# Spread of the row factors in two passes, with the rounded diagonal from ScalarE and its rest from VectorE

## The chip, the cores and the metric

The kernel runs on one core of one Trainium2 chip. The metric is the device time of one execution in microseconds (us). Three runs of the kernel before took 1000.03, 1002.32 and 1002.96 us; their median, 1002.32 us, is its time.

## The reference, cut to what matters

One layer of an encoder: 512 rows of width 1024, all in float32.

```python
def _rms(x, g):
    y = x * lax.rsqrt(jnp.mean(x * x, axis=-1, keepdims=True) + EPS)
    return y * g

x = x + 0.5 * _swiglu(_rms(x, g_ffn1), w_up1, w_down1)      # macaron half-step
h = _rms(x, g_mix)
z = h @ w_in                                                # q, k, v, f, gates
x = x + (gate_a * y_a + gate_b * y_b) @ w_out               # attention and Fourier branches
x = x + 0.5 * _swiglu(_rms(x, g_ffn2), w_up2, w_down2)      # macaron half-step
out = _rms(x, g_final)
```

What matters here is the factor of `_rms`: each of the 512 rows has one number, 1/sqrt(mean of its squares + EPS). The change concerns how that number reaches all 128 partitions.

## The kernel before, in words

**Layout.** `xT` holds x transposed: the model dimension lies on the partitions, the 512 rows along the free dimension. A product therefore has the rows of x as its 512 columns, and the factor of a row has to be known on every partition. The kernel multiplies the raw, gained x (`h_hi`, `h_lo`) by the weights first and applies the factor to the result, in `gate(r, d)` (L1072) and `up(r, d)` (L1078), from the tile `rstd` (128x512, every partition the same).

**Split products.** Operands are split in two: ScalarE rounds (`w_hi`, type float32r, L616), VectorE subtracts (`w_lo`, L1010). TensorE makes three passes for each 128x128 tile: hi by hi (L1556), hi by lo (L1557), and then, once `w_lo` is there, lo by hi (L1568). A granule is 8 such tiles, that is 24 passes of 512 columns. Four slots hold four granules; SP loads granule g when VectorE has split granule g - 4.

**Factors.** There are four norms: `NORM_FFN1` before the first half-step, `NORM_MIX` before the mixer, `NORM_FFN2` before the second half-step, `NORM_FINAL` at the end (it does not use the step changed here). For the first three:

- `sum_squares(n)` on TensorE sums the squares over the partitions into one bank, a row of x on each partition;
- `mean(n)` on VectorE (L1047) makes `var`, GpSimd (L1506) raises it to the power -1/2 and has `rinv`, 128x4: one column for each block of 128 rows;
- `diagonal(n)` on VectorE (L1035) writes `ident * rinv[:, t]` into the four 128-column blocks of `gb_t`;
- `spread_factors(n)` on TensorE (L1599) multiplies a 128x128 tile of ones by it, in plain float32, so that every partition of the bank holds all 512 factors;
- `factors(n)` on VectorE (L1041) copies the bank to `rstd`.

**Where they stand.** The order on each engine is written out by hand. In the half-steps (r = 0 for the first, r = 1 for the second) TensorE runs granules 0 to 3, the `sum_squares` after granule 2 and the `spread_factors` inside granule 3, between its hi passes and its lo passes. Then comes granule 4, which waits until `gate(r, 0)` has read its bank (`out_read`). VectorE's order in `direct_pairs(r)` is

```python
direct_lo(r, 4); mean(nrm); direct_lo(r, 5); diagonal(nrm)
direct_lo(r, 6); factors(nrm); gate(r, 0); up(r, 0); gate(r, 1); up(r, 1); swish(r, 0)
```

ScalarE's order there is `direct_hi` 4, 5 and 6, then `silu(r, 0)` and `silu(r, 1)` (L687), then `direct_hi` 7. In the mixer the granules of f are `f_rows(0)` to `f_rows(3)` (L1772, L1773, L1777); `sum_squares` follows `f_rows(0)`, `spread_factors` follows `f_rows(1)`. There ScalarE splits granule `G_F + 4` after the first and has nothing to do until the second is done.

`gate_t` is the pair `ga_t`, `gb_t`; both are free while the factors are made.

Of the kernel before, what the change touches and what calls it, by code (L numbers as in the profile page):

```python
# [19 lines left out]
F32 = mybir.dt.float32  # L20
F32R = mybir.dt.float32r
ACT = mybir.ActivationFunctionType
ALU = mybir.AluOpType

P = 128
SEQ, D_MODEL, D_FF = 512, 1024, 2816
# [10 lines left out]
TB = SEQ // P  # L37
# [217 lines left out]
def build(nc, io):  # L255
# [9 lines left out]
    with ExitStack() as ctx:  # L265
# [39 lines left out]
        p1_t, _, p1_size = place("p1_t", [P, 2, HALF], F32, ssum_at)  # L305
        u2_t, _, u2_size = place("u2_t", [P, 2, HALF], F32, ssum_at + p1_size)
        u3_t, _, _ = place("u3_t", [P, HALF], F32, ssum_at + p1_size + u2_size)
        ga_t, _, _ = place("ga_t", [P, SEQ], F32)
        gb_t, _, _ = place("gb_t", [P, SEQ], F32)
        ua_t, ua_at, _ = place("ua_t", [P, SEQ], F32)  # L310
        ub_t, _, _ = place("ub_t", [P, SEQ], F32)

# [8 lines left out]
        y_t, _, _ = place("y_t", [P, SEQ], F32)  # L321
        rows = y_t
        ident, _, _ = place("ident", [P, P], F32)
        ones, _, _ = place("ones", [P, P], F32)
        assert at[0] % (TILE_AT // 2) == 0

        a_hi, act_at, a_size = place("a_hi", [P, FK * SEQ], F32R)
# [54 lines left out]
        def sem(name):  # L382
            return ctx.enter_context(nc.semaphore(name))
# [24 lines left out]
        w_lo_ready, h_lo_ready, x_ready = sem("w_lo_ready"), sem("h_lo_ready"), sem("x_ready")  # L408
        out_read, product_ready, a_lo_ready = sem("out_read"), sem("product_ready"), sem("a_lo_ready")
        gain_ready, consts_ready, row_ready = sem("gain_ready"), sem("consts_ready"), sem("row_ready")  # L410
        var_ready, diag_ready, rstd_ready = sem("var_ready"), sem("diag_ready"), sem("rstd_ready")
        proj_lo_ready, v_lo_ready, tab_lo_ready = sem("proj_lo_ready"), sem("v_lo_ready"), sem("tab_lo_ready")
        v_hi_ready = sem("v_hi_ready")
        s_read, max_ready, den_ready, probs_ready = sem("s_read"), sem("max_ready"), sem("den_ready"), sem("probs_ready")
# [199 lines left out]
        def _(act):  # L614
# [3 lines left out]
            def split_hi(g, it=0, n=0):  # L618
# [16 lines left out]
                    act.wait_ge(w_used, g - SLOTS + 1 + n * it)  # L635
                copy(w_hi[:, s, 0:nk, :], raw[:, s, 0:nk, :]).then_inc(w_hi_ready, 1)

            def square_free(n, m):

                if not isinstance(m, int) or m >= 3:  # L640
                    act.wait_ge(sum_added, m + ((DK - 1) * n - 2))
# [14 lines left out]
            act.dma_start(gain_rows[:, :], io["g_ffn1"][0].rearrange("(r p) -> r p", p=P)).then_inc(gain_landed, 16)  # L656
            act.wait_ge(fills_ready, 1)

            nc.scalar.activation(warm[:, :], ones[:, 0:2], ACT.Silu)

            act.wait_ge(gain_ready, 1)

# [17 lines left out]
            def direct_hi(r, j):  # L680

                split_hi(G_UP[r] + j)
# [5 lines left out]

            def direct_pairs(r):

                for j in (4, 5, 6):
                    direct_hi(r, j)
                silu(r, 0)
                silu(r, 1)
                direct_hi(r, 7)
                if r == 0:
                    act.wait_ge(row_ready, 1)
                    act.dma_start(bias_rows, bias_row[:, :]).then_inc(bias_stored, 16)
                t_rounded(r, T_B11)
                direct_hi(r, 8)  # L700
                t_rounded(r, T_1)
                t_rounded(r, T_B21)
                direct_hi(r, 9)
                t_rounded(r, T_2)
                silu(r, 2)
                t_rounded(r, T_4)
                direct_hi(r, 10)
                t_rounded(r, T_3)
                t_rounded(r, T_B22)
                silu(r, 3)  # L710
                direct_hi(r, 11)
                group_hi(r, 0, G0)
                silu(r, 4)
                group_hi(r, 0, G1)
                group_hi(r, 0, G2)
                silu(r, 5)
# [122 lines left out]
            for r in range(2):  # L839
# [19 lines left out]
                for step in mixer_schedule(MIXER_SCALAR):  # L859
                    kind = step[0]  # L860
                    if kind == "f":
                        grp = step[1]
                        if grp == N_FGROUPS - 1:
# [4 lines left out]
                            for nth, i in enumerate((0, 2, 1, 3)):  # L868
                                act.wait_ge(uv_formed, nth + 1)
                                copy(uv_hi[:, i, :], uv_of(i)).then_inc(uv_hi_ready, 1)  # L870
                        split_hi(G_F + grp + SLOTS)
                        if grp == 1:
                            act.wait_ge(tables_landed, 16)
                            copy(tab_hi[:, :], tab_raw[:, :]).then_inc(tab_hi_ready, 1)
# [127 lines left out]
        def _(dve):  # L1002
# [28 lines left out]
            def diagonal(n):  # L1031

                dve.wait_ge(rinv_ready, n + 1)
                for t in range(TB):
                    last = vec.tensor_scalar(gb_t[:, t * P:(t + 1) * P], ident[:, :], rinv[:, t:t + 1], None, ALU.mult)  # L1035
                last.then_inc(diag_ready, 1)

            def factors(n):

# [428 lines left out]
            for h in range(2):  # L1468
# [11 lines left out]
                t = 2 * h  # L1480
# [5 lines left out]
        @block.gpsimd  # L1486
        def _(pool):
            nc.gpsimd.memset(ident[:, :], 0.0).then_inc(ident_ready, 1)
            pool.wait_ge(ident_ready, 1)
            nc.gpsimd.affine_select(out=ident[:, :], in_=ident[:, :], compare_op=ALU.not_equal, fill=1.0, base=0,  # L1490
                                    pattern=[[-1, P]], channel_multiplier=1).then_inc(ident_ready, 1)
            nc.gpsimd.memset(ones[:, :], 1.0).then_inc(fills_ready, 1)
            nc.gpsimd.memset(half[:, :], -0.5).then_inc(fills_ready, 1)
            nc.gpsimd.memset(bias_row[:, :], NEG).then_inc(fills_ready, 1)
            pool.wait_ge(fills_ready, 3)
            for n in range(4):

                for m in range(1, DK - 1 if n == NORM_FINAL else DK):
                    pool.wait_ge(sq_ready, DK * n + m + 1)
                    if m > 1:  # L1500
                        pool.wait_ge(sum_added, (DK - 1) * n + m - 1)
                    nc.gpsimd.tensor_tensor(ssum[:, :], ssum[:, :], sq[:, m % 2, :], ALU.add).then_inc(sum_added, 1)  # L1502
                for i in range(2 if n == NORM_FINAL else 1):
                    blocks = slice(2 * i, 2 * i + 2) if n == NORM_FINAL else slice(0, TB)
                    pool.wait_ge(var_ready, n + 1 + i)
                    nc.gpsimd.tensor_tensor(rinv[:, blocks], var[:, blocks], half[:, blocks],  # L1506
                                            ALU.pow).then_inc(rinv_ready, 1)
                if n in (NORM_FFN1, NORM_FFN2):
                    r = 0 if n == NORM_FFN1 else 1
                    for i, (to, one, two) in enumerate(((T_1, T_B12, T_B11), (T_2, T_B22, T_1), (T_4, T_B21, T_2),  # L1510
                                                        (T_3, T_B22, T_B12))):
                        pool.wait_ge(normed, 2 * HK * r + (HK if to == T_1 else 2 * HK))
                        if i in (1, 2):
                            pool.wait_ge(t_formed, 4 * r + i)
                        nc.gpsimd.tensor_tensor(t_sum[:, to, :, :], t_sum[:, one, :, :], t_sum[:, two, :, :],
                                                ALU.subtract).then_inc(t_formed, 1)
                    for q in range(PAIRS):
                        blk = pair_raw[q % 2]
                        a12, a22 = blk[:, pair_slot(r, G1), 0:HK, :], blk[:, pair_slot(r, G1), HK:DK, :]
                        s2, s3 = blk[:, pair_slot(r, G0), HK:DK, :], blk[:, pair_slot(r, G2), HK:DK, :]  # L1520
                        pool.wait_ge(s13_ready, 2 * (PAIRS * r + q) + 1)
                        nc.gpsimd.tensor_tensor(s2, a22, s3, ALU.subtract).then_inc(s2_ready, 1)  # L1522
                        pool.wait_ge(s2_ready, PAIRS * r + q + 1)
                        nc.gpsimd.tensor_tensor(blk[:, pair_slot(r, G3), 0:HK, :], a12, s2,
                                                ALU.subtract).then_inc(s4_ready, 1)
# [3 lines left out]
        def _(pe):  # L1529
# [56 lines left out]
            def sum_squares(n):  # L1586

                pe.wait_ge(sum_added, (DK - 1) * (n + 1))
                if n == NORM_FFN1:
                    pe.wait_ge(x_ready, DK)  # L1590
                for t in range(TB):
                    mm = nc.tensor.matmul(banks[B_SUM[n]][:, 2 * t:2 * t + 2], ssum[:, t * P:(t + 1) * P], ones[:, 0:2],
                                          start=True, stop=True)
                mm.then_inc(sum_done, 1)

            def spread_factors(n):

                pe.wait_ge(diag_ready, n + 1)
                nc.tensor.matmul(banks[B_RSTD[n]][:, :], ones[:, :], gb_t[:, :], start=True, stop=True).then_inc(rstd_done, 1)  # L1599


            def x_tile(m):
# [9 lines left out]
            def warm_up(count):  # L1612

                for _ in range(count):
                    nc.tensor.matmul(banks[1][:, 0:P], ones[:, :], ones[:, :], start=True, stop=True)

            pe.wait_ge(fills_ready, 1)
            warm_up(6)
# [316 lines left out]
            def finish(h):  # L1935
# [4 lines left out]
                for last_one in (False, True):  # L1940
                    if last_one:
                        pe.wait_ge(last_squared, h + 1)
                    for t in (2 * h, 2 * h + 1):
                        squares = sq[:, 1, t * P:(t + 1) * P] if last_one else ssum[:, t * P:(t + 1) * P]
                        mm = nc.tensor.matmul(banks[B_SUM[NORM_FINAL]][:, 2 * t:2 * t + 2], squares, ones[:, 0:2],
                                              start=not last_one and t == 2 * h, stop=last_one and t == 2 * h + 1)
                mm.then_inc(sum_done, 1)
                pe.wait_ge(last_scaled, h + 1)
# [44 lines left out]
```

## Time and profile before

| | |
|---|---|
| median of three runs | 1002.32 us (1000.03 to 1002.96) |
| profiled execution, whole | 1004.33 us |
| its span, first to last instruction | 1002.5 us |
| mean granted TensorE clock | 0.992 of full speed |
| PE, VectorE, ScalarE, GpSimd busy | 98%, 68%, 44%, 20% of the span |

The profiled execution is one run of its own, so durations are read from it and compared with its own 1004.33 us; the 1.83 us beyond the span lie before the first and after the last instruction. PE is TensorE's matmul side, PEld its weight loads, DVE is VectorE, ACT is ScalarE, POOL is GpSimd, SP issues DMAs. A row of the timeline gives start, duration, engine, line, operation and tiles; "x4" are four instructions merged, with the time from the start of the first to the end of the last. A matmul's record is longer than its share of the array: passes start every 0.23 us while each is shown with 0.39 us. A plain float32 matmul shows as two records.

### The profile page before, as it was taken

The page shows a single profiled execution, that of the slowest core. Times are in us where ns is not written, and L with a number is a line of the kernel's source. Part 1 is how long each engine was busy: PE and PEld are TensorE (multiplying, and loading weights), DVE is VectorE, ACT ScalarE, POOL GpSimd, SP SyncE. Part 2 cuts the span into 40 slices and gives each one's busy share as a digit, 9 for nine tenths or more (in the row PEclk, how much of TensorE's full clock was granted, in tenths as well). Part 3 has the DMA queues.
Part 4 walks back from the last instruction along what each step waited for, and adds up shares of the span by engine and source line. Part 5 has one row for each costly group of instructions (what it writes and reads, how often), then busy time and mean ns, then how long its engine had stood idle before and what let it go on. Part 6 is the DMA issues. An engine that isn't in the chain of part 4 may idle for free.

```text
span 1002.5 us, 16130 instructions
## 1 busy us (share of the span) xinstructions
PE 986.5 (98%) x5780; PEld 876.0 (87%) x5780; DVE 681.4 (68%) x937; ACT 445.2 (44%) x667; POOL 197.8 (20%) x113
## 2 busy tenths in 40 slices
PE   8999999999999999899999999999999999999997
PEld 7789999999888888778888888888999999988887
DVE  6778898989544346568885555468899999953322
ACT  5344444446333234446775343334344444732322
POOL 2453343431011010000000002224233333001101
PEclk9999999999999999899999999999999999999999
DMA  6423333323432363112113343332243432342222
GB/s 212 121 70 105 102 108 99 110 84 90 116 100 89 112 168 117 54 44 83 52 54 108 102 126 104 94 103 58 85 121 90 116 93 84 89 130 87 89 68 84
DMA packets 188743, 98.26 MB, mean 98 GB/s; under 512 B 13384, under 2 KB 186520, under 8 KB 188704
## 3 DMA queue, kind: packets, MB, share of 16 engines
q1 hardware_dynamic: 186912, 94.45, 32.3%
q10 hardware_dynamic: 1792, 3.30, 0.9%
q8 instruction: 24, 0.39, 0.2%
q14 instruction: 15, 0.12, 0.0%
HBM read 95.61 MB, written 2.11 MB: 97 GB/s over the span
## 4 chain that ended last, share of the span: by engine, by line
PE 96%; POOL 1%; DMA 1%; issue 1%; DVE 1%; ACT 1%; SPq 0%; POOLq 0%; ACTq 0%
PE bank L1556 19%; PE bank L1557 19%; PE bank L1568 18%; PE bank L1671 11%; PE bank L1667 11%; PE bank L1665 11%; POOL ssum L1502 1%; PE bank L1871 1%; DMA x_rows<-in_x_dram 1%; PE bank L1772 1%; PE bank L1773 1%; PE bank L1777 1%; PE bank L1886 0%; PE bank L1858 0%; PE bank L1889 0%
## 5 line engine op out<-in xcount | busy, mean ns | idle before, releaser
L616 ACT ACTIVATE w_hi<-raw 128x1024 fp32r<-128x1024 f32 (+2 forms) x202 | 181.3, 901 | 236.9 <-PE bank L1568 148.0
L1010 DVE TENSOR_TENSOR w_lo<-raw,w_hi 128x1024 fp32r<-128x1024 f32 (+2 forms) x138 | 149.9, 1089 | 141.7 <-ACT w_hi L616 140.1
L1667 PE MATMUL bank<-t_lo,w_hi 128*128 128x256 f32 x896 | 224.7, 283 | 0.0
L1665 PE MATMUL bank<-t_hi,w_hi 128*128 128x256 f32 x896 | 224.6, 283 | 0.0
L1667 PEld LDWEIGHTS bank<-t_lo,w_hi 128*128 128x128 f32 x896 | 172.0, 192 | 0.2
L1665 PEld LDWEIGHTS bank<-t_hi,w_hi 128*128 128x128 f32 x896 | 172.0, 192 | 0.2
L1502 POOL TENSOR_TENSOR ssum<-ssum,sq 128x512 f32<-128x512 f32 x27 | 41.2, 1524 | 525.6 <-ACT sq L653 524.8
L1671 PE MATMUL bank<-t_hi,w_lo 128*128 128x256 f32 x896 | 144.0, 283 | 0.0
L1556 PE MATMUL bank<-a_hi,w_hi 128*128 128x512 f32 (+1 forms) x374 | 140.1, 379 | 0.0
L1557 PE MATMUL bank<-a_lo,w_hi 128*128 128x512 f32 (+1 forms) x374 | 139.4, 377 | 0.0
L1671 PEld LDWEIGHTS bank<-t_hi,w_lo 128*128 128x128 f32 x896 | 123.6, 192 | 0.0
L1178 DVE TENSOR_TENSOR w_lo<-raw,w_hi 128x1024 fp32r<-128x1024 f32 x64 | 90.9, 1420 | 9.3 <-ACT w_hi L616 9.3
L616 ACT ACTIVATE w_hi<-raw_b 128x1024 fp32r<-128x1024 f32 x64 | 60.8, 949 | 80.0 <-POOL raw_b L1522 40.3
L1178 DVE TENSOR_TENSOR w_lo<-raw_b,w_hi 128x1024 fp32r<-128x1024 f32 x64 | 92.8, 1450 | 3.8 <-ACT w_hi L616 3.7
L1568 PE MATMUL bank<-a_hi,w_lo 128*128 128x512 f32 (+1 forms) x374 | 91.1, 377 | 0.0
L1556 PEld LDWEIGHTS bank<-a_hi,w_hi 128*128 128x128 f32 x374 | 70.4, 188 | 12.9
L1557 PEld LDWEIGHTS bank<-a_lo,w_hi 128*128 128x128 f32 x374 | 70.4, 188 | 12.6
L1568 PEld LDWEIGHTS bank<-a_hi,w_lo 128*128 128x128 f32 x374 | 67.8, 188 | 12.9
L1556 PE MATMUL bank<-hf_hi,w_hi 128*128 128x512 f32 x192 | 76.5, 399 | 0.0
L1557 PE MATMUL bank<-hf_lo,w_hi 128*128 128x512 f32 x192 | 75.8, 395 | 0.0
L1556 PE MATMUL bank<-h_hi,w_hi 128*128 128x512 f32 x176 | 70.3, 399 | 0.4 <-issue 0.4
L1557 PE MATMUL bank<-h_lo,w_hi 128*128 128x512 f32 x176 | 69.9, 397 | 0.0
(238 smaller groups left out, 1488.1 us busy)
## 6 DMA issues: line engine op xcount, KB each, us to landing
raw<-in_w_down_dram SPq DMA_DIRECT2D x48, 384.0 KB, 3.0
raw_b<-in_w_up_dram SPq DMA_DIRECT2D x64, 256.0 KB, 3.7
raw<-in_w_up_dram SPq DMA_DIRECT2D x64, 256.0 KB, 3.6
raw<-in_w_up_dram SPq DMA_DIRECT2D x24, 512.0 KB, 3.8
raw<-in_w_in_dram SPq DMA_DIRECT2D x22, 512.0 KB, 3.7
raw<-in_w_down_dram SPq DMA_DIRECT2D x32, 128.0 KB, 2.2
raw<-in_w_out_dram SPq DMA_DIRECT2D x8, 512.0 KB, 3.4
x_rows<-in_x_dram SPq DMA_DIRECT2D x4, 512.0 KB, 7.9
```

What stands on the lines that cost most here:

```text
L616: return nc.scalar.activation(dst, src, ACT.Copy, scale=scale)
L1010: vec.tensor_tensor(w_lo[:, s, 0:nk, :], raw[:, s, 0:nk, :], w_hi[:, s, 0:nk, :].bitcast(F32), ALU.subtract).then_inc(w_lo_ready, 1)
L1178: vec.tensor_tensor(w_lo[:, slot, 0:nk, :], pair_raw[q % 2][:, slot, 0:nk, :], w_hi[:, slot, 0:nk, :].bitcast(F32), ALU.subtract).then_inc ...
L1502: nc.gpsimd.tensor_tensor(ssum[:, :], ssum[:, :], sq[:, m % 2, :], ALU.add).then_inc(sum_added, 1)
L1556: nc.tensor.matmul(out_ap, w_hi[:, s, k, :], xh, start=first and i == 0, stop=False)
L1557: mm = nc.tensor.matmul(out_ap, w_hi[:, s, k, :], xl, start=False, stop=False)
L1568: mm = nc.tensor.matmul(out_ap, w_lo[:, s, k, :], x_parts(k)[0], start=False, stop=last and i == len(tiles) - 1)
L1665: nc.tensor.matmul(out_ap, w_hi[:, slot, at_ + k, :], hi[:, k, :], start=first and k == 0, stop=False, skip_group_check=not first)
L1667: nc.tensor.matmul(out_ap, w_hi[:, slot, at_ + k, :], lo_[:, k, :], start=False, stop=False, skip_group_check=not first)
L1671: mm = nc.tensor.matmul(out_ap, w_lo[:, slot, at_ + k, :], hi[:, k, :], start=False, stop=k == HK - 1, skip_group_check=not first)
L1772: nc.tensor.matmul(o_ap, rows_of(h_hi, k, t), group_of_four(w_hi, slot, kk), start=k == 0, stop=False)
L1773: nc.tensor.matmul(o_ap, rows_of(h_lo, k, t), group_of_four(w_hi, slot, kk), start=False, stop=False)
```

## The change

The diagonal is made twice. ScalarE writes `ident * rinv` rounded to float32r into `diag_hi` (in the place of `ga_t`); VectorE writes the rest, `ident * rinv - diag_hi`, into `diag_lo` (in the place of `gb_t`). TensorE multiplies the ones, now of type float32r, by each, in one pass each that add up in the bank, in place of one float32 product. The second pass waits for the rest. In ScalarE's order the new step stands between `direct_hi` 5 and `direct_hi` 6 in both half-steps, and after the split of `G_F + 4` in the mixer. VectorE's step stays where it was and now waits for ScalarE's too. Other uses of the ones read them as float32, as before.

```diff
+        diag_hi, _, _ = place("diag_hi", [P, SEQ], F32R, ga_at)
+        diag_lo, _, _ = place("diag_lo", [P, SEQ], F32R, gb_at)
...
-        ones, _, _ = place("ones", [P, P], F32)
+        ones_r, _, _ = place("ones_r", [P, P], F32R)
...
+            def diagonal_hi(n):
+
+                act.wait_ge(rinv_ready, n + 1)
+                for t in range(TB):
+                    last = copy(diag_hi[:, t * P:(t + 1) * P], ident[:, :], scale=rinv[:, t:t + 1])
+                last.then_inc(diag_hi_ready, 1)
...
             def direct_pairs(r):
 
-                for j in (4, 5, 6):
-                    direct_hi(r, j)
+                direct_hi(r, 4)
+                direct_hi(r, 5)
+                diagonal_hi(NORM_FFN1 if r == 0 else NORM_FFN2)
+                direct_hi(r, 6)
                 silu(r, 0)
                 silu(r, 1)
                 direct_hi(r, 7)
...
                         split_hi(G_F + grp + SLOTS)
+                        if grp == 0:
+                            diagonal_hi(NORM_MIX)
...
             def diagonal(n):
 
                 dve.wait_ge(rinv_ready, n + 1)
+                dve.wait_ge(diag_hi_ready, n + 1)
                 for t in range(TB):
-                    last = vec.tensor_scalar(gb_t[:, t * P:(t + 1) * P], ident[:, :], rinv[:, t:t + 1], None, ALU.mult)
-                last.then_inc(diag_ready, 1)
+                    block = slice(t * P, (t + 1) * P)
+                    last = vec.scalar_tensor_tensor(out=diag_lo[:, block], in0=ident[:, :], scalar=rinv[:, t:t + 1],
+                                                    in1=diag_hi[:, block].bitcast(F32), op0=ALU.mult, op1=ALU.subtract)
+                last.then_inc(diag_lo_ready, 1)
...
             def spread_factors(n):
 
-                pe.wait_ge(diag_ready, n + 1)
-                nc.tensor.matmul(banks[B_RSTD[n]][:, :], ones[:, :], gb_t[:, :], start=True, stop=True).then_inc(rstd_done, 1)
+                pe.wait_ge(diag_hi_ready, n + 1)
+                nc.tensor.matmul(banks[B_RSTD[n]][:, :], ones_r[:, :], diag_hi[:, :], start=True, stop=False)
+                pe.wait_ge(diag_lo_ready, n + 1)
+                nc.tensor.matmul(banks[B_RSTD[n]][:, :], ones_r[:, :], diag_lo[:, :], start=False, stop=True).then_inc(rstd_done, 1)
```

## Rows read from the trace of the kernel before

**Rows 1.** The page's first part: busy time, share and instructions of each engine

```profile
PE 986.5 (98%) x5780; PEld 876.0 (87%) x5780; DVE 681.4 (68%) x937; ACT 445.2 (44%) x667; POOL 197.8 (20%) x113
```

**Rows 2.** The page's fourth part: the chain that ended last, by engine

```profile
PE 96%; POOL 1%; DMA 1%; issue 1%; DVE 1%; ACT 1%; SPq 0%; POOLq 0%; ACTq 0%
```

**Rows 3.** Waits of PE over the whole span: total us, times, longest

```profile
PE bank L1533 <- DVE y_t L1362: 2.3, 1, 2.3
```

**Rows 4.** Timeline of all engines around the spread of the second half-step

```profile
655.89 1.98 PE L1568 MATMUL bank<-hf_hi,w_lo 128*128 128x512 f32 x8
...
657.96 1.06 ACT L616 ACTIVATE w_hi<-raw 128x1024 fp32r<-128x1024 f32 x1 [4.38 <-PE bank L1568]
...
658.93 1.93 POOL L1506 TENSOR_TENSOR rinv<-var,half 128x4 f32<-128x4 f32 x1 [12.54 <-DVE var L1047]
659.04 1.28 ACT L687 ACT_TABLE_LOAD   x1
...
660.89 0.87 DVE L1035 TENSOR_SCALAR gb_t<-ident,rinv 128x128 f32<-128x128 f32 x4 [0.91 <-POOL rinv L1506]
...
661.68 1.22 DVE L1010 TENSOR_TENSOR w_lo<-raw,w_hi 128x1024 fp32r<-128x1024 f32 x1
...
662.28 1.02 PE L1599 MATMUL bank<-gb_t,ones 128*128 128x512 f32 x2
...
662.74 2.43 PE L1568 MATMUL bank<-hf_hi,w_lo 128*128 128x512 f32 x8
...
663.34 0.69 DVE L1041 COPY rstd<-bank 128x512 f32<-128x512 f32 x1 [0.44 <-PE bank L1599]
664.06 0.69 DVE L1072 TENSOR_TENSOR ga_t<-bank,rstd 128x512 f32<-128x512 f32 x1
...
665.00 0.40 PE L1556 MATMUL bank<-hf_hi,w_hi 128*128 128x512 f32 x1
```

**Rows 5.** Timeline around the spread of the first half-step

```profile
28.15 3.88 ACT L616 ACTIVATE w_hi<-raw 128x1024 fp32r<-128x1024 f32 x4
...
32.77 1.94 POOL L1506 TENSOR_TENSOR rinv<-var,half 128x4 f32<-128x4 f32 x1 [2.37 <-DVE var L1047]
...
37.52 1.02 PE L1599 MATMUL bank<-gb_t,ones 128*128 128x512 f32 x2
...
37.98 2.40 PE L1568 MATMUL bank<-hf_hi,w_lo 128*128 128x512 f32 x8
...
40.21 0.42 PE L1556 MATMUL bank<-hf_hi,w_hi 128*128 128x512 f32 x1
```

**Rows 6.** Timeline around the spread of the mixer

```profile
372.97 1.02 POOL L1506 TENSOR_TENSOR rinv<-var,half 128x4 f32<-128x4 f32 x1 [4.43 <-DVE var L1047]
...
376.64 1.02 PE L1599 MATMUL bank<-gb_t,ones 128*128 128x512 f32 x2
...
377.74 0.40 PE L1773 MATMUL bank<-w_hi,h_lo 128*128 128x512 f32 x1
```

**Rows 7.** ScalarE's groups by form: busy us and mean ns, then idle before

```profile
L616 ACT ACTIVATE w_hi<-raw 128x1024 fp32r<-128x1024 f32 x106 | 111.7, 1056 | 132.1 <-PE bank L1568 49.0 <-PE bank L1671 43.4 <-POOL raw L1522 25.1
...
L616 ACT ACTIVATE w_hi<-raw 128x512 fp32r<-128x512 f32 x48 | 29.6, 618 | 7.0 <-PE bank L1568 6.9
...
L616 ACT ACTIVATE hf_hi<-xT,consts 128x512 fp32r<-128x512 f32 x8 | 5.8, 723 | 25.8 <-DVE xT L1262 25.8
```

**Rows 8.** VectorE's groups by form, with the same columns

```profile
L1020 DVE SCALAR_TENSOR_TENSOR hf_lo<-xT,consts,hf_hi 128x512 fp32r<-128x512 f32 x8 | 6.0, 751 | 7.0 <-ACT hf_hi L616 7.0
...
L1361 DVE TENSOR_TENSOR y_t<-cos_t,bank 128x128 f32<-128x128 f32 x8 | 2.3, 281 | 0.1
```

**Rows 9.** Windows: from:to, length, busy by engine, PEclk, DMA share, GB/s

```profile
33.00:38.00 5.00, 5.00 (x17) 3.76 (x15) 2.83 (x6) 0.00 (x0) 1.71 (x1) 0.66 0.97 287
412.00:420.00 8.00, 6.84 (x20) 5.49 (x21) 4.01 (x12) 2.88 (x7) 0.00 (x0) 0.57 0.18 54
...
424.00:427.00 3.00, 0.99 (x9) 0.79 (x7) 2.92 (x4) 1.98 (x5) 0.00 (x0) 1.00 0.17 47
```

More of the change, by code:

```diff
@@ L307, in build @@
         u3_t, _, _ = place("u3_t", [P, HALF], F32, ssum_at + p1_size + u2_size)
-        ga_t, _, _ = place("ga_t", [P, SEQ], F32)
-        gb_t, _, _ = place("gb_t", [P, SEQ], F32)
+        ga_t, ga_at, _ = place("ga_t", [P, SEQ], F32)
+        gb_t, gb_at, _ = place("gb_t", [P, SEQ], F32)
+        diag_hi, _, _ = place("diag_hi", [P, SEQ], F32R, ga_at)
+        diag_lo, _, _ = place("diag_lo", [P, SEQ], F32R, gb_at)
         ua_t, ua_at, _ = place("ua_t", [P, SEQ], F32)
@@ L410, in build @@
         gain_ready, consts_ready, row_ready = sem("gain_ready"), sem("consts_ready"), sem("row_ready")
-        var_ready, diag_ready, rstd_ready = sem("var_ready"), sem("diag_ready"), sem("rstd_ready")
+        var_ready, rstd_ready = sem("var_ready"), sem("rstd_ready")
+        diag_hi_ready, diag_lo_ready = sem("diag_hi_ready"), sem("diag_lo_ready")
         proj_lo_ready, v_lo_ready, tab_lo_ready = sem("proj_lo_ready"), sem("v_lo_ready"), sem("tab_lo_ready")
@@ L657, in _ @@
             act.wait_ge(fills_ready, 1)
-            nc.scalar.activation(warm[:, :], ones[:, 0:2], ACT.Silu)
+            nc.scalar.activation(warm[:, :], ones_r[:, 0:2].bitcast(F32), ACT.Silu)
             act.wait_ge(gain_ready, 1)
@@ L1491, in _ @@
                                     pattern=[[-1, P]], channel_multiplier=1).then_inc(ident_ready, 1)
-            nc.gpsimd.memset(ones[:, :], 1.0).then_inc(fills_ready, 1)
+            nc.gpsimd.memset(ones_r[:, :].bitcast(F32), 1.0).then_inc(fills_ready, 1)
             nc.gpsimd.memset(half[:, :], -0.5).then_inc(fills_ready, 1)
@@ L1591, in sum_squares @@
                 for t in range(TB):
-                    mm = nc.tensor.matmul(banks[B_SUM[n]][:, 2 * t:2 * t + 2], ssum[:, t * P:(t + 1) * P], ones[:, 0:2],
+                    mm = nc.tensor.matmul(banks[B_SUM[n]][:, 2 * t:2 * t + 2], ssum[:, t * P:(t + 1) * P], ones_r[:, 0:2].bitcast(F32),
                                           start=True, stop=True)
@@ L1614, in warm_up @@
                 for _ in range(count):
-                    nc.tensor.matmul(banks[1][:, 0:P], ones[:, :], ones[:, :], start=True, stop=True)
+                    nc.tensor.matmul(banks[1][:, 0:P], ones_r[:, :].bitcast(F32), ones_r[:, :].bitcast(F32), start=True, stop=True)
             pe.wait_ge(fills_ready, 1)
@@ L1944, in finish @@
                         squares = sq[:, 1, t * P:(t + 1) * P] if last_one else ssum[:, t * P:(t + 1) * P]
-                        mm = nc.tensor.matmul(banks[B_SUM[NORM_FINAL]][:, 2 * t:2 * t + 2], squares, ones[:, 0:2],
+                        mm = nc.tensor.matmul(banks[B_SUM[NORM_FINAL]][:, 2 * t:2 * t + 2], squares, ones_r[:, 0:2].bitcast(F32),
                                               start=not last_one and t == 2 * h, stop=last_one and t == 2 * h + 1)
```

## The prediction, made before the changed kernel was run

> **What bounds the kernel now.** I read the page's busy shares first: TensorE is busy 98% of the span, no other engine above 68% [rows 1]. The chain that ended last is TensorE for 96% [rows 2]. So what counts is TensorE's time, and what other engines do counts only where TensorE waits for it. The waits of PE come third: the dearest on another compute engine is one of 2.3 us in the mixer [rows 3], and none lies at the three places that the change touches. Then the timeline of those three places, since a wait that is not there now may be there afterwards; it shows how close the present order is. In the second half-step `gate` ends at 664.06 + 0.69 = 664.75 us and granule 4, which waits for it, starts at 665.00 [rows 4]: 0.25 us of room, no more. Last the windows, for the granted clock.
>
> **TensorE's saving.** Passes of 512 columns start every (1.98 - 0.39)/7 = 0.227 us at full clock (eight passes of L1568 in 1.98 us, the last one's record 0.39) [rows 4]. The float32 product in the second half-step starts at 662.28. Behind it stand eight passes and then granule 4's first at 665.00: 2.72 us, of which the eight passes are 1.82, so the product holds the array for 0.90 us. In the first half-step the same sum is 40.21 - 37.52 - 1.82 = 0.87 [rows 5], in the mixer 377.74 - 376.64 - 0.23 = 0.87 [rows 6]. Two float32r passes take 0.45. The saving is at most 0.42 us at each place, 1.3 us in all, if nothing is late.
>
> **The new instructions.** They are four ScalarE copies of 128 columns with a scale from a tile, and four scalar_tensor_tensor of 128 columns on VectorE in place of four tensor_scalar. The trace shows neither form.
> ScalarE: the copy with such a scale is 723 ns at 512 columns; a column costs (1056 - 618)/512 = 0.86 ns [rows 7]; for 128 columns that gives 0.723 - 384 x 0.00086 = 0.395 us. Instructions back to back overlap by (4 x 1.056 - 3.88)/3 = 0.115 [rows 5, 7]. Four take 4 x 0.395 - 3 x 0.115 = 1.24 us.
> VectorE: 0.751 at 512 columns; a column of a two-tensor operation costs (1.22 - 0.281)/896 = 1.05 ns (w_lo of 1024, y_t of 128) [rows 4, 8], which gives 0.348 for 128. The overlap is (4 x 0.281 - 0.87)/3 = 0.085, taking a tensor_scalar at y_t's 281 ns [rows 4, 8]. Four take 1.14 us.
> The bounds for each four are 0.87, which the present four take, and four 512-column instructions end to end, 2.9 and 3.0 us. I stay with 1.24 and 1.14, since the 128-column rows are the nearest.
> The Trainium skill ("VectorE: DVE Perf Modes", section "The DRAIN you can't avoid") says that the next VectorE instruction starts only when the pipe is empty, which speaks against cutting work in four. Here four of about 281 ns end after 0.87 us, so the trace shows some overlap [rows 4, 8]. Without any overlap the eight would take 2.97 us in place of 2.38, and the second half-step would lose 0.6 us more.
>
> The two fours lie one behind the other: `rinv`, then ScalarE 1.24, then VectorE 1.14; before, only 0.87 lay there. Behind the new ScalarE step stands `direct_hi` 6, which so far ran long before; behind VectorE's stand `direct_lo` 6, the copy to `rstd`, and `gate`.
>
> **First half-step.** `rinv` ends at 34.71 [rows 5]. Rounded diagonal 34.76 to 36.00, rest 36.03 to 37.17. TensorE wants them at 37.52 and 37.75: no stall, since it runs at a reduced clock just before (0.66 mean over 33 to 38 us) [rows 9]. `w_hi` 6 is ready at 36.95, `w_lo` 6 at 38.3, the copy starts at 38.2 (the second pass ends at 37.75 + 0.39), `gate` about 0.73 later (as 663.34 to 664.06) [rows 4] and ends at 39.64; with 0.2 for hand-over and restart of TensorE, granule 4 can start at 39.84. By TensorE's own work it would be 39.79. Before it was 40.21. Term: -0.37 us. If the diagonals are cheaper, -0.42; at the far end (VectorE 3.0) +2.
>
> **Mixer.** `rinv` ends at 373.99 [rows 6]; diagonals ready at 375.3 and 376.45, wanted at 376.64 and 376.87. Behind ScalarE's wait stands the split of the next granule, which waits for TensorE's end of `f_rows(1)` anyway. Term: -0.42 us; its cover is 0.4 us thick, and it turns to +1.3 at the far end.
>
> **Second half-step.** Here TensorE runs at full clock and the cover is gone. `rinv` ends at 660.86 [rows 4]. Rounded diagonal to 662.14, rest from 662.17 to 663.31. TensorE wants the rest at 662.28 + 0.23 = 662.51 and stalls until about 663.4: 0.9 us, half of it paid by the saving. But that is not what ends last. `w_hi` 6, which before ran at 657.96, now ends at 663.1. `w_lo` 6 starts behind the rest, 663.23, and ends at 664.45 (before 662.90); copy from 664.37; `gate` 665.09 to 665.77; granule 4 with the 0.2 at 665.97 in place of 665.00. Term: +0.97 us, nothing of the saving left. With 0.87 for each four it is +0.5; with no overlap +1.6; at the far end +3.3 with VectorE's 3.0. The table load of 1.28 us that followed `w_hi` 6 at 659.04 now runs from 663.1 to 664.4, still ahead of `gate`'s end: no cost [rows 4]. The SP load that waits for `w_lo` 6 comes 1.6 us later, for a granule four granules of 24 x 0.227 = 5.4 us away: no cost. No wait of PE follows in this half-step before its last rows, so nothing gives the time back: all engines there move with TensorE.
>
> **Sum.** -0.37 - 0.42 + 0.97 = +0.2 us. On the profiled execution's own time that is 1004.33 + 0.2 = 1004.5; on the median of the runs, which lies 2 us lower, 1002.5 us. The bounds of the costs alone give -0.3 (each four 0.87) to about +6.6 (the three far ends), and +1.2 when only the overlap is missing.
>
> **Rivals.**
> A. Nothing is late in the second half-step, since ScalarE starts its four earlier or does them much faster than its rows say: 1.3 us are saved, 1001.0 us. For it: TensorE is the bound. Against: even 0.87 for each four leaves the rest late, at 662.6, and `gate` behind it. 0.08.
> B. Slower: the stall of 0.9 us and the one at granule 4 behind it put TensorE at half clock, as it is in 412 to 420 us after the wait in the mixer. There the granted clock is 0.57 (a mean over the two levels, 2.4 and 1.2 GHz), and (1 - 0.57) x 8 = 3.4 us of full-speed work are lost [rows 3, 9]. It would give 1002.5 + 3.4 = 1005.9. Against: in 424 to 427 TensorE is busy for only 0.99 us of 3 and keeps its full clock [rows 9]. It decides from the point where a short stall is followed by a second one. 0.07. The Trainium skill ("TensorE: Matmul & The Clock Gate", section "HAM oscillation — how this bites in real kernels") has idle gaps bring the half clock back. The trace shows both outcomes.
> C. The other way round: a stretch at half clock falls away because work has shifted by half a microsecond. The stretch around 33 to 38 us costs (1 - 0.66) x 5 = 1.7 us, the one in the mixer 3.4 [rows 9]: 999 to 1001 us. The three runs of the kernel before lie 2.9 us apart, so something of this size comes and goes by itself. 0.05.
> D. The float32r passes of the spread cost as much as the float32 product. Then the savings are gone, 0.8 us more: 1003.3. Against: all other float32r passes of that size start every 0.227 us. 0.02.
> The forecast's own case has the remaining 0.78.
>
> **How the numbers follow.** A measurement of this kernel can hardly tell less than 0.3%, that is 3 us, from no change. The forecast, A and D are all within it. Only B, half of C, and the far ends of the new instructions' costs leave it. Faster 0.05, same 0.87, slower 0.08. The range has to hold the spread of the kernel itself (1.5 us each way), A below, and part of B above: 999.8 to 1005.2.
>
> **What would show it.** In the trace of the changed kernel: two records of about 0.39 us in place of the two that take 1.02, at all three places; in the mixer and the first half-step no wait of PE on `diag_lo`; in the second half-step a wait of nearly 1 us on `diag_lo`, then about 0.3 us on `gate`'s tile before granule 4, which starts some 1 us later relative to `rinv`'s end (4.14 us before, 5.1 after). ScalarE's four should take 1.24 us and VectorE's 1.14. The prediction is wrong if the second half-step shows no wait, or if the granted clock differs in some stretch after the new stall.

## The result and the profile after

The changed kernel takes 1004.96 us (median of 20 runs, 1001.81 to 1007.25), the kernel before 1002.66 us (20 runs, 1000.03 to 1003.4). The ratio is 1.0024, 95% interval 1.0017 to 1.0032. The forecast was 1002.5 us and no measurable change. The time is inside the stated range and the ratio inside the 0.3% that was called no change, but the sign is clear: it is 2.3 us slower, and 0.2 were forecast.

TensorE's waits in the changed kernel (engine and line, what it waited for, total us, times, longest us):

```profile
PE bank L1550 <- DVE y_t L1379: 2.3, 1, 2.3
...
PE bank L1618 <- DVE diag_lo L1051: 1.5, 2, 0.8
...
PE bank L1573 <- DVE ga_t L1089: 0.4, 2, 0.2
```

The first row answers to [rows 3] and is unchanged. The other two are new: the second pass of the spread (L1618) waits twice for the rest of the diagonal, and granule 4 waits twice for `gate`'s tile. Both happen in both half-steps, not in the second alone as forecast.

The second half-step after, which answers to [rows 4]:

```profile
658.76 1.93 POOL L1523 TENSOR_TENSOR rinv<-var,half 128x4 f32<-128x4 f32 x1 [12.54 <-DVE var L1064]
...
660.73 1.28 ACT L619 ACTIVATE diag_hi<-ident,rinv 128x128 fp32r<-128x128 f32 x4 [7.31 <-POOL rinv L1523]
...
661.91 1.04 ACT L619 ACTIVATE w_hi<-raw 128x1024 fp32r<-128x1024 f32 x1
...
662.12 1.14 DVE L1051 SCALAR_TENSOR_TENSOR diag_lo<-ident,rinv,diag_hi 128x128 fp32r<-128x128 f32 x4 [2.31 <-ACT diag_hi L619]
662.97 1.28 ACT L697 ACT_TABLE_LOAD   x1
663.18 1.22 DVE L1024 TENSOR_TENSOR w_lo<-raw,w_hi 128x1024 fp32r<-128x1024 f32 x1
...
663.32 0.50 PE L1618 MATMUL bank<-diag_lo,ones_r 128*128 128x512 f32 x1 [0.76 <-DVE diag_lo L1051]
663.65 2.02 PE L1585 MATMUL bank<-hf_hi,w_lo 128*128 128x512 f32 x8
664.31 0.69 DVE L1058 COPY rstd<-bank 128x512 f32<-128x512 f32 x1
665.03 0.69 DVE L1089 TENSOR_TENSOR ga_t<-bank,rstd 128x512 f32<-128x512 f32 x1
...
665.86 0.49 PE L1573 MATMUL bank<-hf_hi,w_hi 128*128 128x512 f32 x1 [0.19 <-DVE ga_t L1089]
```

Read it as a chain: `rinv` ends at 660.69, ScalarE's four follow, then VectorE's four, then `w_lo` of granule 6, which stands behind them in VectorE's order (`w_hi` 6, made after ScalarE's diagonal, was ready 0.23 us earlier, at 662.95); then the copy, `gate`, and granule 4. From `rinv`'s end to granule 4 it is 5.17 us; before it was 4.14.

The first half-step after, which answers to [rows 5]:

```profile
32.76 1.94 POOL L1523 TENSOR_TENSOR rinv<-var,half 128x4 f32<-128x4 f32 x1 [2.37 <-DVE var L1064]
...
36.06 0.50 PE L1616 MATMUL bank<-diag_hi,ones_r 128*128 128x512 f32 x1
...
37.31 0.50 PE L1618 MATMUL bank<-diag_lo,ones_r 128*128 128x512 f32 x1 [0.74 <-DVE diag_lo L1051]
37.65 2.00 PE L1585 MATMUL bank<-hf_hi,w_lo 128*128 128x512 f32 x8
...
39.86 0.49 PE L1573 MATMUL bank<-hf_hi,w_hi 128*128 128x512 f32 x1 [0.21 <-DVE ga_t L1089]
40.19 0.39 PE L1574 MATMUL bank<-hf_lo,w_hi 128*128 128x512 f32 x1
```

5.16 us, the same to 0.01. Against this one execution of the kernel before (5.50 us in [rows 5]) that looks like a gain. It is not one, as the windows show; first 33 to 38 us, then 412 to 420, with the granted clock third from the right:

```profile
33.00:38.00 5.00, 4.26 (x18) 3.00 (x17) 2.69 (x6) 2.23 (x5) 1.70 (x1) 1.00 0.98 284
412.00:420.00 8.00, 6.88 (x21) 5.40 (x22) 3.43 (x9) 2.70 (x7) 0.00 (x0) 0.57 0.09 28
```

Here TensorE ran the first half-step at full clock (1.00), there at 0.66 [rows 9]. The mixer after, which answers to [rows 6]:

```profile
372.69 1.02 POOL L1523 TENSOR_TENSOR rinv<-var,half 128x4 f32<-128x4 f32 x1 [4.44 <-DVE var L1064]
...
376.36 0.39 PE L1616 MATMUL bank<-diag_hi,ones_r 128*128 128x512 f32 x1
376.58 0.39 PE L1618 MATMUL bank<-diag_lo,ones_r 128*128 128x512 f32 x1
...
377.04 0.39 PE L1792 MATMUL bank<-w_hi,h_lo 128*128 128x512 f32 x1
```

The two passes start 0.22 us apart without a wait, and the second pass of the next granule starts 0.68 us after the spread did; before it was 1.10. That is the saving of 0.42 us, as computed.

### The profile page after: what moved, and what is told of

It reads as the page before. It is cut to its first block, busy times and chain, and to the rows that moved or that the text cites. A ratio compares the mean times of both kernels' runs of the same rounds, so it can differ in the third digit from the quotient of the medians.

```text
span 1003.4 us, 16145 instructions
## 1 busy us (share of the span) xinstructions
PE 985.1 (98%) x5780; PEld 874.3 (87%) x5780; DVE 682.0 (68%) x937; ACT 448.9 (45%) x679; POOL 197.9 (20%) x113
## 4 chain that ended last, share of the span: by engine, by line
PE 94%; DVE 2%; POOL 1%; issue 1%; ACT 1%; DMA 1%; SPq 0%; POOLq 0%; ACTq 0%; DVEq 0%
PE bank L1573 19%; PE bank L1574 18%; PE bank L1585 18%; PE bank L1690 11%; PE bank L1686 11%; PE bank L1684 11%; PE bank L1890 1%; POOL ssum L1519 1%; DMA x_rows<-in_x_dram 1%; PE bank L1791 1%; PE bank L1792 1%; PE bank L1796 1%; DVE w_lo L1024 1%; PE bank L1905 0%; PE bank L1877 0%
```

## The experiments

Theory 1: the longer chain behind `rinv` (two fours one behind the other, granule 6 behind them) costs 1.0 us in the second half-step and, where TensorE is at full clock, more in the first; the mixer saves 0.4. Theory 2: more stretches at half clock. Theory 3: the whole loss sits in the second half-step.

**The change in the mixer alone, twice.** The half-steps keep the float32 product.

```diff
+        TWO_PASS = (NORM_MIX,)
...
             def spread_factors(n):
+                if n not in TWO_PASS:
+                    pe.wait_ge(diag_ready, nth_of(False, n))
+                    nc.tensor.matmul(banks[B_RSTD[n]][:, :], ones_r[:, :].bitcast(F32), gb_t[:, :], start=True, stop=True).then_inc(rstd_done, 1)
+                    return
-                pe.wait_ge(diag_hi_ready, n + 1)
+                pe.wait_ge(diag_hi_ready, nth_of(True, n))
...
```

`TWO_PASS` names the norms that keep the change, and `nth_of` counts the spreads of either kind. ScalarE's and VectorE's steps are chosen in the same way, here and in the next three kernels.

> The change in the mixer alone; both half-steps keep the float32 product. Theory 1 (waits): the loss lies in the half-steps, where the two diagonals stand one behind the other ahead of granule 4. Then granule 4 starts in both as before (4.1 us after rinv's end in the second), the mixer's spread takes 0.45 us in place of 0.87, and the time is that of the kernel before less 0.4 us, about 1002.2 us. Theory 2 (clock): the loss comes from more stretches at half clock, set off by the changed spread wherever it stands; then this kernel too is slower, by 1 to 2 us, with more of such stretches in its trace.

> The kernel of mixer_only once more, on this chip, to see whether it beats the kernel before: 0.4 us less than before by its trace, ratio 0.9996; the first measurement gave 0.9992. Theory 2 (clock) has it at or above 1.

Measured: ratios 0.9992 (0.9983 to 1.0001, 1001.79 us) and 0.9995 (0.9986 to 1.0004, 1002.18 us). Both intervals hold 1, so no gain is shown by the times; a loss of 0.1 to 0.2% there, as by theory 2, is excluded.

**The change in the half-steps alone.**

> The change in the two half-steps alone; the mixer keeps the float32 product. Theory 1: a wait of about 0.75 us on the rest of the diagonal in the second half-step and, where TensorE is at full clock there, in the first too; each is followed by a short wait for gate's tile; granule 4 starts about 1.0 us later in the second and 1.3 us later in the first. Time: the kernel before plus 2.3 us, 1005.0 us (plus 0.6 if the first runs at half clock there). Theory 2: no more than the changed kernel's +2.3, with no fixed relation to the waits.

Measured: 1.0031 (1.0019 to 1.0043), 1005.08 us, from 6 runs. The loss is all there.

**In the second alone, and in the first alone.**

> The change in the second half-step alone. Theory 1 (waits): from rinv's end to granule 4's start it is 5.2 us there (4.1 with the float32 product); the first half-step, with its float32 product, takes 5.5 us where TensorE is at half clock and about 4.2 at full clock. Time: the kernel before plus 1.0 us, about 1003.6 us. Theory 3 (the whole loss sits in the second half-step): plus 2.5 us.

> The change in the first half-step alone. My prediction took it for a gain of 0.37 us, read from an execution that was at half clock there. Theory 1: at full clock it is a loss of 1.0 us (5.2 us from rinv's end to granule 4 in place of 4.2), at half clock a gain of 0.4; over the runs plus 0.5 to 1.0 us, about 1003.3 us. The prediction's term: about 1002.2 us. Theory 3: no change.

Measured: second 1.0008 (1.0000 to 1.0017), first 1.0013 (1.0005 to 1.0022), 1003.55 us each. Theory 3 falls, and so does the prediction's term of -0.37 us for the first half-step. In the kernel with the change in the second alone the first half-step has the float32 product, and this time TensorE was at full clock in it:

```profile
32.97 1.94 POOL L1534 TENSOR_TENSOR rinv<-var,half 128x4 f32<-128x4 f32 x1 [2.37 <-DVE var L1075]
...
36.12 1.02 PE L1628 MATMUL bank<-gb_t,ones_r 128*128 128x512 f32 x2
36.57 2.42 PE L1596 MATMUL bank<-hf_hi,w_lo 128*128 128x512 f32 x8
...
38.83 0.39 PE L1584 MATMUL bank<-hf_hi,w_hi 128*128 128x512 f32 x1
39.06 0.40 PE L1585 MATMUL bank<-hf_lo,w_hi 128*128 128x512 f32 x1
```

`rinv` ends at 34.91 and granule 4 starts 3.92 us later. Its second pass follows its first after 0.23 us. Where granule 4 had to wait for `gate`'s tile, in the changed kernel, it follows after 0.33 (39.86 to 40.19): a pass that has waited keeps the array 0.1 us longer. The lengths to the start of granule 4 do not contain this, and it comes on top once in each half-step. In the kernel with the change in the first alone TensorE was at half clock there (0.70 over 33 to 38 us):

```profile
32.11 1.94 POOL L1534 TENSOR_TENSOR rinv<-var,half 128x4 f32<-128x4 f32 x1 [2.37 <-DVE var L1075]
...
36.85 0.39 PE L1631 MATMUL bank<-diag_hi,ones_r 128*128 128x512 f32 x1
...
37.08 0.39 PE L1633 MATMUL bank<-diag_lo,ones_r 128*128 128x512 f32 x1
...
39.21 0.49 PE L1584 MATMUL bank<-hf_hi,w_hi 128*128 128x512 f32 x1
```

5.16 us, with no wait on the rest. So the four cases of the first half-step are: float32 product 5.50 at half clock, 3.92 at full; two passes 5.16 at half clock, 5.16 at full. With two passes in this order the other engines set the length, and TensorE's clock there does not change it.

**Granule 6 ahead of the diagonals.**

```diff
                 direct_hi(r, 5)
-                diagonal_hi(NORM_FFN1 if r == 0 else NORM_FFN2)
                 direct_hi(r, 6)
+                diagonal_hi(NORM_FFN1 if r == 0 else NORM_FFN2)
...
-                diagonal(nrm)
                 direct_lo(r, 6)
+                diagonal(nrm)
```

> The whole change, but both splits of granule 6 stand ahead of the diagonals, on ScalarE and on VectorE. Tells the two links of the new chain apart. Theory 1: the wait on the rest of the diagonal stays (about 0.75 us), but the copy to rstd no longer queues behind w_lo 6: it starts 0.5 us earlier, gate's wait before granule 4 goes, and each half-step gets back 0.4 us. Time about 1004.2 us against 1005.0 of the changed kernel. If the queue behind w_lo 6 is not what ends last, nothing is gained.

Measured: 1.0017 (1.0005 to 1.0030), 1004.79 us, which the times do not tell from the changed kernel's 1.0024. The trace does, in the second half-step:

```profile
657.23 1.93 POOL L1523 TENSOR_TENSOR rinv<-var,half 128x4 f32<-128x4 f32 x1 [12.54 <-DVE var L1064]
...
661.78 0.50 PE L1618 MATMUL bank<-diag_lo,ones_r 128*128 128x512 f32 x1 [0.76 <-DVE diag_lo L1051]
...
662.31 0.69 DVE L1058 COPY rstd<-bank 128x512 f32<-128x512 f32 x1 [0.59 <-PE bank L1618]
...
663.98 0.39 PE L1573 MATMUL bank<-hf_hi,w_hi 128*128 128x512 f32 x1
```

The wait on the rest stays, the copy now waits for TensorE instead of queuing behind `w_lo` 6, the wait of granule 4 is gone, and it starts 4.82 us after `rinv`: 0.35 of the 1.03 us come back, and the 0.1 us of the first pass. The first half-step has 4.79. The gain forecast in its time, 0.8 us, is not shown by the times.

**The factor split first, both diagonals at once** (with granule 6 ahead as well).

```diff
+                vec.tensor_copy(rinv_hi[:, :], rinv[:, :]).then_inc(parts_ready, 1)
...
+                vec.tensor_tensor(rinv_lo[:, :], rinv[:, :], rinv_hi[:, :].bitcast(F32), ALU.subtract).then_inc(parts_ready, 1)
...
-                    last = vec.scalar_tensor_tensor(out=diag_lo[:, block], in0=ident[:, :], scalar=rinv[:, t:t + 1],
-                                                    in1=diag_hi[:, block].bitcast(F32), op0=ALU.mult, op1=ALU.subtract)
+                    last = vec.tensor_scalar(diag_lo[:, block], ident[:, :], rinv_lo[:, t:t + 1], None, ALU.mult)
```

ScalarE scales by `rinv_hi` as soon as it is there.

> As granule6_first, and the 128x4 factors are split into a rounded part and a rest first, by two small VectorE instructions; then ScalarE writes the rounded diagonal and VectorE the rest at the same time (tensor_scalar in place of scalar_tensor_tensor). Theory 1: both diagonals are ready about 1.7 us after rinv in place of 2.5; at full clock the second pass waits 0 to 0.3 us, and granule 4 is no later than in the kernel before. All three spreads keep most of the 0.42 us: 1001.6 to 1002.4 us. Theory 2: as slow as the changed kernel.

Measured: 0.9997 (0.9988 to 1.0006), 1002.18 us. The second half-step:

```profile
656.90 1.93 POOL L1528 TENSOR_TENSOR rinv<-var,half 128x4 f32<-128x4 f32 x1 [12.54 <-DVE var L1069]
...
659.20 1.28 ACT L622 ACTIVATE diag_hi<-ident,rinv_hi 128x128 fp32r<-128x128 f32 x4 [2.21 <-DVE rinv_hi L1051]
659.40 0.88 DVE L1057 TENSOR_SCALAR diag_lo<-ident,rinv_lo 128x128 fp32r<-128x128 f32 x4
...
660.53 0.50 PE L1621 MATMUL bank<-diag_hi,ones_r 128*128 128x512 f32 x1
660.87 0.40 PE L1623 MATMUL bank<-diag_lo,ones_r 128*128 128x512 f32 x1
...
662.93 0.42 PE L1578 MATMUL bank<-hf_hi,w_hi 128*128 128x512 f32 x1
```

4.10 us in both half-steps at full clock. The loss is gone in the second and 0.18 us of it are left in the first (3.92 with the float32 product), with the two fours side by side and granule 6 ahead. But the time was forecast to hold most of the 0.42 us at all three places, and in the second half-step only 0.04 us of it are there. ScalarE's four start 0.37 us after `rinv`, behind the small split, and take 1.28 us, so the first pass starts 1.70 us after `rinv`; the float32 product, where nothing waited, started after 1.42 in the second half-step (662.28 in [rows 4]) and after 1.21 in the first (36.12 above).

**The passes alone.** This kernel leaves out the rest of the diagonal, so its factors are rounded. ScalarE's step and the waits on it are left out too.

```diff
-                    last = vec.scalar_tensor_tensor(out=diag_lo[:, block], ...)
+                    last = vec.tensor_scalar(diag_lo[:, block], ident[:, :], rinv[:, t:t + 1], 0.5, ALU.mult, ALU.mult)
...
-                nc.tensor.matmul(banks[B_RSTD[n]][:, :], ones_r[:, :], diag_hi[:, :], start=True, stop=False)
+                nc.tensor.matmul(banks[B_RSTD[n]][:, :], ones_r[:, :], diag_lo[:, :], start=True, stop=False)
                 nc.tensor.matmul(banks[B_RSTD[n]][:, :], ones_r[:, :], diag_lo[:, :], start=False, stop=True)
```

> The two passes alone, without the longer chain: VectorE writes one diagonal, rounded and halved, by tensor_scalar (the same four instructions of 0.87 us as before), and TensorE adds it twice. ScalarE has no part in it, and the rest of the diagonal is left out, so the factors have the precision of one rounded part. Theory 1: nothing waits, and each spread saves about 0.4 us: no wait of PE on the diagonal, 3.7 us from rinv's end to granule 4 in the second half-step, 1001.4 us. If float32r passes cost what the float32 product costs, 1002.6 us.

Measured: 0.9989 (0.9980 to 0.9998), 1001.35 us, with this in the second half-step, where `rinv` ends at 657.83:

```profile
659.25 0.39 PE L1611 MATMUL bank<-diag_lo,ones_r 128*128 128x512 f32 x1
659.48 0.39 PE L1612 MATMUL bank<-diag_lo,ones_r 128*128 128x512 f32 x1
659.71 1.98 PE L1580 MATMUL bank<-hf_hi,w_lo 128*128 128x512 f32 x8
...
661.52 0.43 PE L1568 MATMUL bank<-hf_hi,w_hi 128*128 128x512 f32 x1
```

3.69 us in place of 4.14, and 5.09 in the first half-step, partly at half clock, where the float32 product has 5.50. The saving that the change is after exists, 0.45 and 0.4 us here; it is the chain ahead of it that eats it.

**Both kernels again.** The sum of the parts (+0.13, +0.08, -0.07%) is 1.4 us and the whole was 2.3 (both half-steps together had +0.31% by themselves, 0.19 to 0.43), so the whole and its base were measured again.

> The changed kernel once more. Its parts measured alone add up to +0.13% and +0.08% for the half-steps and -0.07% for the mixer, some 1.4 us, and the whole measured +2.3. Theory 1 (waits): from rinv's end to granule 4 it is again 5.2 us in both half-steps, at either clock; what differs between its executions is the start and the mixer's stretch at half clock. The ratio is then 1.0010 to 1.0024. Theory 2 (clock): the ratio is again 1.0024 or more, and the trace shows more or longer stretches at half clock than those of the kernel before.

> The kernel before once more, against itself: a ratio of 1.0000 within its interval, which tells how far two measurements of one kernel differ. Theory 1: from rinv's end to granule 4 it is 5.5 us in the first half-step if TensorE is at half clock there and 3.9 us if not, and 4.1 us in the second.

> The changed kernel a third time, for its trace alone. Theory 1: 5.2 us in both half-steps again; the same number of stretches at half clock as in the other traces, one or two beside the start. Theory 2: more of them.

> The kernel before a third time, for its trace alone. Theory 1: 5.5 or 3.9 us in the first half-step by the clock, 4.1 us in the second. Theory 2: fewer stretches at half clock than in the changed kernel.

Measured: the changed kernel 1.0023 (1.0011 to 1.0035), 1004.45 us; the kernel before against itself 1.0007 (0.9998 to 1.0015). The two single executions took 1005.71 and 1004.11 us. The lengths from `rinv`'s end to granule 4 repeat to 0.02 us, in the first half-step at like clock:

| trace | clock at 33 to 38 us | first half-step | second |
|---|---|---|---|
| before (the profile) | 0.66 | 5.50 | 4.14 |
| before, again / third | 1.00 / 1.00 | 3.91 / 3.91 | 4.14 / 4.15 |
| changed | 1.00 | 5.16 | 5.17 |
| changed, again / third | 1.00 / 1.00 | 5.17 / 5.17 | 5.17 / 5.17 |
| mixer alone / again | 0.73 / 1.00 | 5.51 / 3.92 | 4.14 / 4.13 |
| half-steps alone | 0.85 | 5.15 | 5.16 |
| first alone | 0.70 | 5.16 | 4.14 |
| second alone | 1.00 | 3.92 | 5.16 |
| granule 6 ahead | 1.00 | 4.79 | 4.82 |
| factor split first | 1.00 | 4.10 | 4.10 |
| passes alone | 0.88 | 5.09 | 3.69 |

The same three traces of each kernel, cut at these points over their whole spans, show where the difference lies (us):

| stretch | before | changed | difference of the means |
|---|---|---|---|
| start to `rinv` of the first half-step | 34.71, 34.11, 35.19 | 34.70, 34.22, 34.96 | -0.05 |
| to granule 4 | 5.50, 3.91, 3.91 | 5.16, 5.17, 5.17 | +0.72 |
| to `rinv` of the mixer | 333.78, 333.76, 333.75 | 333.86, 333.86, 333.87 | +0.10 |
| to `rinv` of the second half-step | 286.86, 287.74, 287.78 | 286.98, 288.61, 287.13 | +0.11 |
| to granule 4 | 4.14, 4.14, 4.15 | 5.17, 5.17, 5.17 | +1.02 |
| to the end | 337.54, 337.50, 337.52 | 337.58, 337.61, 337.62 | +0.08 |

That is 2.0 us in all. The two stretches behind granule 4 hold the 0.1 us of its first pass. The mixer's holds the saving of 0.42 us, and varies by more than that between executions of one kernel.

Theory 2 is not ruled out as an addition, but it has little room. In all 14 traces the clock is below full only before 38 us, between 409 and 431 us and in the last 6 us. The stretches there do differ between traces; the changed kernel's second trace has one more at 424 to 430 us, at the end of TensorE's wait of 2.3 us on VectorE's `fy_lo` in the mixer, where its third has none (windows of the second, then of the third):

```profile
424.00:430.00 6.00, 3.70 (x14) 2.96 (x13) 4.05 (x9) 2.12 (x5) 0.00 (x0) 0.72 0.30 87
```

```profile
424.00:430.00 6.00, 3.70 (x22) 3.16 (x21) 4.73 (x9) 2.80 (x6) 0.00 (x0) 1.00 0.30 87
```

The same stretch stands at 0.72 and 0.75 in the second and third trace of the kernel before. Over 32 runs of the changed kernel the mean granted clock is 0.9931, over the 23, 26 and 35 runs of the kernel before that stood beside the experiments 0.9946, 0.9944 and 0.9942. A thousandth is 1.0 us of full-speed work. But the 11 runs of the kernel before, measured as an experiment, have 0.9931 too, at 1003.1 us, and among the 32 runs of the changed kernel the time does not go with this clock: the five at 0.995 took 1005.8 to 1006.3 us, the seven at 0.991 took 1003.7 to 1006.4.

## Why the prediction was right and where it was wrong

**The new instructions** were sized well: ScalarE's four 1.28 us (1.24 foretold), one of them 391 ns (395); VectorE's four 1.14 (1.14), one 348 ns (348). The overlap is there too: four of 348 ns end after 1.14 us, not 1.39. The section of the Trainium skill that the prediction names ("VectorE: DVE Perf Modes", section "The DRAIN you can't avoid") also says that a next instruction that is not held starts earlier, which the prediction left out; the trace agrees with this exception.

**TensorE's saving** of 0.42 us for each spread holds: 0.42 in the mixer, 0.45 in the kernel with the passes alone.

**The second half-step**: +0.97 foretold, +1.03 measured in the trace (5.17 less 4.14), by the chain as written: the wait on the rest (0.76 us), then `gate` behind `w_lo` 6. Moving granule 6 ahead gave back the second link, running the fours side by side the first. The 0.1 us of the waiting first pass is in neither number.

**The first half-step is the step that failed.** The prediction said: "no stall, since it runs at a reduced clock just before". That half clock belonged to the one execution that was profiled; other executions of the kernel do not have it. In 9 of the 14 traces of this study TensorE is at full clock there, in all three of the changed kernel too. At full clock the term is 5.16 - 3.92 = +1.24 us, not -0.37. The bounds of the instructions' costs gave this term +2 at its far end, for a reason that did not come true; that the cover itself might be missing was not among them. The range did not come from these bounds either, but from the kernel's own spread and the rivals A and B. That it holds the measured 1004.96 us, and that the ratio stays within the 0.3%, is owed to this width, not to the sum.

**The sum.** The prediction's +0.2 us lacks the 1.6 us between +1.24 and -0.37, and the 0.1 us by which the first pass of granule 4 is longer after its wait, once in each half-step. With full clock in the first half-step it is 1.24 + 1.03 - 0.42 + 0.2 = +2.05 us; against an execution of the kernel before that is at half clock there it is -0.34 + 1.03 - 0.42 + 0.2 = +0.5 us. With half clock in 5 of 14, as in the traces, it would be 9/14 x 1.24 - 5/14 x 0.34 + 1.03 - 0.42 + 0.2 = +1.5 us. Measured: 2.3 (1.7 to 3.2) and 2.3 (1.1 to 3.5). The waits thus account for 1.5 to 2.05 us. The rest, 0.3 to 0.8 us, is less than either interval is wide, and not settled. In the three traces of each kernel it lies in the mixer: there one of the changed kernel's, 288.61 us, has 3.4 us more at half clock than any of the other five, and without it the means differ by -0.40 us, the saving. Whether the change brings such a stretch about or the runs merely fell so, no experiment here tells; no stretch at half clock follows the new waits themselves in any of the three traces (1.00 over 33 to 38 us, and over 658 to 667).

**The rivals.** A (nothing late) is what the kernel with the passes alone shows, 1001.35 us against 1001.0: the price was about right, the condition was not met. B (the new stalls put TensorE at half clock) is refuted where it was placed: from the second half-step's stall on the clock is full up to the last 6 us, in all three traces. C (a stretch falls away) describes what single executions do, in both kernels; it gave no gain over the runs. D (passes as dear as the product) is refuted by 3.69 against 4.14 us.

## What to carry to other kernels

A cheaper operation on the engine that bounds the kernel is worth only what the chain that feeds it allows: here 0.42 us saved stood against diagonals that are ready 2.53 us after their start (660.73 to 663.26) in place of 0.87, with 0.25 us of room. When work is split into a rounded part and a rest, split the small operand (128x4) first, so that two engines can form the large parts side by side; with that, and with granule 6 ahead, the second half-step took no longer than before and the first 0.18 us longer. And when a cost is said to be hidden, ask whether the cover is in every execution: half clock in a profile is a cover that may not be there.

## What the runs showed of the hardware

The stretch at half clock early in the kernel (33 to 38 us) is present in some executions of the same program and absent in others: 0.66 and 1.00 in three traces of the kernel before, where the part behind it takes 5.50 or 3.91 us. And a reduced clock can be free: with the two passes this part takes 5.16 us at either clock, because ScalarE and VectorE set its length.

A pass that has waited costs more than its share. At full clock a pass of 512 columns is followed by the next after 0.23 us; after a wait it is 0.33 to 0.34 us, at every wait on `diag_lo` and on `gate`'s tile in the three traces of the changed kernel (for example 663.32 to 663.65, and 39.86 to 40.19).
